# Two-block sequence model on one core: rms norms at the head, between the blocks and at the layer ends rearranged, residual input loaded twice

## What is computed

```python
def rmsnorm(x, g):
    return x * lax.rsqrt(jnp.mean(x * x, axis=-1, keepdims=True) + 1e-6) * g

h = concatenate([meta, x])                     # first block
xn = rmsnorm(h, norm_g)                        # its sections: xn @ w_in
h = h + merged @ w_out
x = rmsnorm(h, final_norm_g)[:, 16:]           # norm 1 between the blocks

h = concatenate([meta_2, x])                   # second block, two layers
u = rmsnorm_2(h, pre_norm_w[l])                # norm 2 between the blocks, when l = 0
h = h + rmsnorm_2(mix @ w_out_2[l], post_norm_w[l])
```

## Time and profile before

| | us |
|---|---|
| median of 3 runs | 3834.13 |
| lowest, highest | 3829.82, 3835.44 |
| the profiled execution, device time | 3825.8 |
| its span in the trace | 3824.0 |
| PE busy | 3630.4 (95%) |
| DVE busy | 1438.7 (38%) |
| ACT busy | 463.9 (12%) |

### The profile page before, as it was taken

The page is one execution under the profiler, slowest core; times in us unless marked ns, Lnnn a source line. Parts: engine busy times, 40 slices in busy tenths (PEclk is TensorE's granted clock), DMA queues, the critical chain, the costliest instruction groups (busy, mean ns, idle before and its releaser), DMA issues.

```text
span 3824.0 us, 46727 instructions
## 1 busy us (share of the span) xinstructions
PE 3630.4 (95%) x19871; PEld 3020.2 (79%) x19871; DVE 1438.7 (38%) x2423; ACT 463.9 (12%) x951; POOL 19.0 (0%) x42
## 2 busy tenths in 40 slices
PE   7999999999999999979999989899789999899997
PEld 5888888888888988868878867677678888777786
DVE  0335431324375534210204654634202026546341
ACT  1011200011011101010000012111100000111111
POOL 0000000000000000000000000000000000000000
PEclk9999899999999999989999999999999999899998
DMA  6442244442434114524444422333424444322431
GB/s 208 139 154 88 86 135 132 135 130 94 155 122 131 47 47 164 181 88 132 132 135 145 140 89 73 98 108 110 144 88 154 135 138 148 101 83 78 129 110 66
DMA packets 424736, 456.29 MB, mean 119 GB/s; under 512 B 14621, under 2 KB 402030, under 8 KB 423758
## 3 DMA queue, kind: packets, MB, share of 16 engines
q1 hardware_dynamic: 422382, 443.19, 36.4%
q0 software_dynamic: 1824, 8.28, 0.6%
q10 hardware_dynamic: 352, 2.23, 0.2%
HBM read 449.35 MB, written 4.33 MB: 119 GB/s over the span
## 4 chain that ended last, share of the span: by engine, by line
PE 90%; DVE 4%; ACT 2%; DVEq 2%; issue 1%; ACTq 0%; DMA 0%; POOL 0%; POOLq 0%
PE bank L1591 32%; PE bank L276 21%; PE bank L350 9%; PE bank L1718 8%; PE bank L383 4%; PE bank L1790 3%; PE bank L1005 3%; DVE tok L431 1%; PE bank L527 1%; PE bank L307 1%; PE bank L1683 1%; PE bank L1777 1%; PE bank L315 1%; PE bank L1666 1%; PE bank L1700 1%
## 5 line engine op out<-in xcount | busy, mean ns | idle before, releaser
L1591 PE MATMUL bank<-xnT,ring 128*128 128x272 f32 (+3 forms) x5632 | 1291.8, 392 | 19.7 <-DVEq L331 19.7
L1591 PEld LDWEIGHTS bank<-xnT,ring 128*128 128x128 f32 (+2 forms) x5632 | 1058.5, 189 | 250.6 <-issue 35.1
L276 PE MATMUL bank<-xnT,ring 128*128 128x272 f32 (+1 forms) x3072 | 690.0, 388 | 11.6 <-DVEq L331 10.9
L276 PEld LDWEIGHTS bank<-xnT,ring 128*128 128x128 f32 x3072 | 585.3, 191 | 115.8 <-issue 13.4
L350 PE MATMUL bank<-xnT,ring 128*128 128x256 f32 x1536 | 345.5, 385 | 0.7 <-ACT wk L1179 0.7
L350 PEld LDWEIGHTS bank<-xnT,ring 128*128 128x128 f32 x1536 | 292.9, 193 | 41.4 <-ACT wk L1179 1.1
L1718 PE MATMUL bank<-G,ring 128*128 128x272 f32 (+1 forms) x1024 | 242.6, 388 | 1.3 <-DVE G L2135 1.3
L1718 PEld LDWEIGHTS bank<-G,ring 128*128 128x128 f32 x1024 | 193.0, 190 | 38.9 <-issue 3.6
L383 PE MATMUL bank<-G,ring 128*128 128x256 f32 x768 | 169.6, 385 | 9.8 <-DVEq L651 5.0
L383 PEld LDWEIGHTS bank<-G,ring 128*128 128x128 f32 x768 | 148.2, 193 | 31.0 <-DVEq L651 5.4
L431 DVE RECIPROCAL G<-G 128x272 f32<-128x272 f32 (+3 forms) x25 | 149.4, 5977 | 1.8
(11 more groups left out here) (456 smaller groups left out, 2656.6 us busy)
## 6 DMA issues: line engine op xcount, KB each, us to landing
ring<-in_w_in SPq DMA_DIRECT2D x156, 2048.0 KB, 8.2
ring<-in_w_out SPq DMA_DIRECT2D x32, 2048.0 KB, 8.4
ring<-in_w_br SPq DMA_DIRECT2D x12, 2048.0 KB, 8.1
ring<-in_w_out SPq DMA_DIRECT2D x16, 1024.0 KB, 11.1
kept<-hT POOLq DMA_DIRECT2D x1, 2176.0 KB, 10.1
hT<-kept POOLq DMA_DIRECT2D x1, 2176.0 KB, 11.9
wk<-in_pool_w POOLq DMA_DIRECT2D x2, 1024.0 KB, 11.1
out<-G SPq DMA_DIRECT2D x2, 1024.0 KB, 5.0
```

The source lines that it names most:

```text
L276: mm = pe.matmul(bank[j][:, first:T], ring[:, s, k, j * P:(j + 1) * P], rhs[:, k, first:T], start=(k == 0), stop=(k == KT - 1))
L1591: mm = pe.matmul(out_, ring[:, s, k, c:c + m], xnT[:, k, first:T], start=(k == 0), stop=(k == KT - 1))
```

## The change

1. **Head.** `x` comes in as rows of 128 tokens (`x_tok`), half by SP and half by ACT, `meta` apart (`m_tok`). The 14 vectors are loaded by POOL. ACT sums the squares of each row while squaring (`accum_out`), DVE does half of the second 128 rows. The norm's factor of each token stands on a diagonal (`diag`), and one matmul of a tile of `x_tok` with it turns and scales at once; DVE multiplies by the gain straight out of PSUM. PE makes the turned tile k+2 between the steps k of the first output tile of the first section (`chasing_section_pe`).
2. **Residual.** No store and no load of `hT`. `x` is loaded again to `x_tok` (`x_back`) by POOL after `rk_free`, and two matmuls with `eye` add it to each tile of `merged @ w_out` in PSUM.
3. **Between the blocks.** ACT squares each tile and copies it to `hT`. DVE keeps two running sums: of the squares, and of the squares times `final_norm_g` squared. Two matmuls each turn the running sums and the last tile into two rows, from which both norms' factors follow. DVE writes `xnT` straight from `hT` with both gains (`gpre`), one `xn_ready` per tile, PE chases, and the 16 products for `hT` come after. The meta tokens' norm and the vectors' transposes stand inside the section, at tiles 4 and 8.
4. **Layer ends and the head of layer 1.** The squares are summed on DVE as well; PE has two matmuls instead of 16 (`acc_own`). PE chases in the first section of layer 1. `Ln` reads PSUM itself, with epsilon as bias, so the DVE step of L324 is gone.

The core of the diff:

```diff
+        def chasing_section_pe(pe, first, ready):
+            for s in range(SLOTS):
+                pe.wait_ge(w_loaded[s], 16 * uses["pe"][s].go())
+                for j in range(2):
+                    pe.wait_ge(proj_free, tiles["pe"].go())
+                    for k in range(KT):
+                        if s == j == 0:
+                            ready(k)
+                        mm = pe.matmul(bank[j][:, first:T], ring[:, s, k, j * P:(j + 1) * P], xnT[:, k, first:T],
+                                       start=(k == 0), stop=(k == KT - 1))
...
         def rms_root_act(act, first=0):
...
+            act.preload_act_table(ACT.Ln)
+            act.activation(row, norm_bank(act)[:, first:T], ACT.Ln, bias=eps[:, 0:1]).then_inc(work_free, 1)
...
-            v.tensor_scalar(sm[:, first:T], b[:, first:T], 1.0 / D, EPS, ALU.mult, ALU.add).then_inc(work_free, 1)
...
+        def block_end_pe(pe):
...
+                for k in range(KT):
+                    pe.matmul(bank[j][:, META:T], ring[:, s, k, j * P:(j + 1) * P], merged[:, k, META:T],
+                              start=(k == 0), stop=False)
+                if t == 0:
+                    pe.wait_ge(S["x_back"], 32)
+                for i in range(2):
+                    mm = pe.matmul(bank[j][:, META + i * P:META + (i + 1) * P], x_tok[i][:, t * P:(t + 1) * P], eye,
+                                   start=False, stop=(i == 1))
...
+                if t == 8:
+                    pe.wait_ge(S["meta_sq"], 1)
+                    for k in range(KT):
+                        mm = pe.matmul(banks["meta"][:, 0:META], ones, squares1[:, k, 0:META], start=(k == 0), stop=(k == KT - 1))
...
+            pe.wait_ge(S["rms_acc"], count["pe"]["rms_acc"].go())
+            for name, acc in (("own", acc_own), ("both", acc_both)):
+                pe.matmul(banks[name][:, META:T], ones, acc[:, META:T], start=True, stop=False)
...
+        def block_end_act(act):
...
+                act.activation(squares1[:, t, META:T], bank[t % 2][:, META:T], ACT.Square, scale=SQ).then_inc(S["rms_sq"], 1)
+                act.activation(hT[:, t, META:T], bank[t % 2][:, META:T], ACT.Copy).then_inc(proj_free, 1)
...
+            act.preload_act_table(ACT.Ln)
+            act.wait_ge(S["rows_in"], 1)
+            act.activation(l_row[:, META:T], c_row[:, META:T], ACT.Ln)
+            act.wait_ge(S["rows_in"], 2)
+            act.activation(n_row[:, META:T], n_row[:, META:T], ACT.Ln, bias=eps[:, 0:1]).then_inc(S["rms_rstd"], 1)
+            act.drain()
+            act.activation(sm[:, META:T], l_row[:, META:T], ACT.Exp, scale=-0.5)
+            act.wait_ge(S["rows_in"], 3)
+            act.activation(c_row[:, META:T], c_row[:, META:T], ACT.Exp, scale=-0.5).then_inc(S["rms_rstd"], 1)
...
+            v.tensor_scalar(c, wbank(work["dve"].n)[:, META:T], EPS, None, ALU.add).then_inc(work_free, 1)
...
+            v.reciprocal(n, c)
...
+            v.tensor_tensor(n, wbank(work["dve"].n)[:, META:T], n, ALU.mult).then_inc(work_free, 1)
...
-                        if 4 * s + j >= 2:
-                            rms_tile_pe(pe, squares, 4 * s + j - 2, m0)
...
+                wait("rms_acc")
+                pe.matmul(b[:, m0:T], ones, acc_own[:, m0:T], start=True, stop=False)
+                wait("rms_sq", KT)
+                pe.matmul(b[:, m0:T], ones, squares[:, KT - 1, m0:T], start=False, stop=True).then_inc(work_full, 1)
...
+            sp.dma_start(x_tok[0], x[0, 0:P, :]).then_inc(S["x0_in"], 16)
...
-            pool.dma_start(kept, flat(hT)).then_inc(S["h_kept"], 16)
...
+                    pool.dma_start(tok[row:row + rows, n * P:(n + 1) * P], src).then_inc(S["stack_in"], 16)
...
+            def turned_input(k):
+                u = turns["pe"].go()
+                pe.wait_ge(turn_free, u)
+                for (t0, n), src, d in zip(TOK_AT, x_tok + [m_tok], diag):
+                    mm = pe.matmul(tbank(u)[:, t0:t0 + n], src[0:n, k * P:(k + 1) * P], d[0:n, 0:n], start=True, stop=True)
+                mm.then_inc(turn_full, 1)
+
+            def input_ready(k):
+                if k + 2 < KT:
+                    turned_input(k + 2)
+                pe.wait_ge(turn_free, k + 3)
...
+            act.activation(junk[0:META, 0:D], m_tok, ACT.Square, scale=SQ, accum_out=ssq[0:META, 3:4]).then_inc(S["x_sq"], 1)
...
+            for i in range(2):
+                v.tensor_scalar(diag[i], eye, rstd3[:, i:i + 1], None, ALU.mult)
...
+            for k in range(KT):
+                v.wait_ge(turn_full, k + 1)
+                v.tensor_scalar(xnT[:, k, :], tbank(k + 1)[:, 0:T], vec("norm_g", 1, k), None, ALU.mult).then_inc(turn_free, 1)
```

354 lines of the change are left out of this document (229 added, 125 removed).

## The result

The changed kernel takes 3765.5 us, the median of four runs from 3763.3 to 3767.4, against 3832.0 for the kernel before beside it: a ratio of 0.983, with a 95% interval from 0.981 to 0.984. The forecast was 3780.6 with a range from 3766 to 3793, so the sign was right and the gain larger than the range allowed. The profiled execution took 3763.3 with a span of 3761.6, against a span of 3824.0 before: 62.4 us shorter, where the sum said 53.5.

The account below looks back on a forecast made before the run. PE bounds the kernel (90% of the last-ending chain). Gains of 10.7 (head), 24.5 (between blocks), 11.5 (layer ends) and 6.8 (layer 1's head) sum to 53.5 us; 3834.1 less that gives 3780.6, range 3766 to 3793.

Parts of the forecast that it names:

- `x` matmuls: Residual in the 16 `w_out` tiles: 32 added PE matmuls with 128 moving columns cost 10.2 us, bounds 6.9 and 11.4.
- The head: Program start to the first output tile: it ends at 44.7 against 55.4, gain 10.7 us, bounds 4 and 17.
- the turned tile: Head: two matmuls with 128 moving columns and one with 16 take 0.90 us, 14.4 for 16 tiles.
- the start at the low clock: Head: cost 1.7 us before the change; the prediction took 2.0.
- Rows 8: Profile rows of the first mixer: four records, two 128-column matmuls, take 0.64 us, used to price small matmuls.
- rival (a): Weight loads hide better: 0.107 per 128-column record, `x` matmuls 6.9 us, turned tile 0.60; total 3772.5; chance 0.14.
- Between the blocks otherwise: Last `w_out` tile to layer 0: pause 47.9 becomes 7.5 us; gain 24.5 after added PE work, bounds 21 and 30.
- Layer ends and the head of layer 1: 13 sums of squares leave PE per layer, gain 11.5 us; layer 1 starts after 3.0 instead of 9.82, gain 6.8.
- Clock: Head of layer 1: clock might stay up over the shorter pause; counted as nothing, worth up to 2.6 us more.
- (b): Head: input lands no earlier, `x` at 16.3, gain 6.4 or nothing, total up to 3791 us; chance 0.10.
- (c): Layer starts: PE waits for several products or DVE falls behind; 2 x 6.3 us lost, total 3793; chance 0.03.
- (d): Head: POOL's small vector loads run one after another, there at 80 us; total 3839 to about 3920; chance 0.02.

Follow-up runs that it names:

- warm_head: Changed kernel plus 20 spare PE matmuls before the vectors and 9 before the first turned tile: 3760.7 us; the same code again 3767.6 us.
- sums_on_pe: Changed kernel with the layer-end sums of squares back on PE, one matmul between output tiles, without DVE's running sum: 3776.8 us.
- one_wait: Changed kernel, but PE waits for all 16 `xn_ready` before the first matmul of layers 0 and 1: 3778.5 us.
- after_again: The changed kernel run once more, unchanged: 3770.2 us.
- warm_early: Changed kernel with only 20 spare matmuls before PE's first wait, none later: 3766.7 us.
- warm_late: Changed kernel with only 4 spare matmuls between the vectors' transposes and the first turned tile: 3768.0 us.
- meta_twice: Changed kernel with each turned tile of the head doing its 16-token matmul a second time: 3782.6 us.
- warm_pauses: Changed kernel plus spare matmuls in three pauses: between the blocks, around layer 1's norm sums, before the output transposes: 3762.6 us.
- three best kernels: Changed kernel with early head fill, meta tokens loaded first and pauses filled; then plus best2's addition; then plus best3's: 3754.7, 3751.4, 3746.6 us.
- meta_dve: Changed kernel with the meta tokens' squares added by one DVE reduction, leaving PE one matmul of 2 records: 3765.6 us.
- best2: Changed kernel with warm_early's fill, meta tokens loaded before x's second half, warm_pauses' fills and meta_dve's reduction: 3751.4 us.
- best3: best2 with 6 more spare matmuls between the vectors' transposes and the first turned tile: 3746.6 us.

## Why the forecast was too high

The median came out 15.1 us below the forecast. 4.0 of it are the basis: 3834.1 was the median of three executions, and 28 of the same kernel have 3830.1. 1.2 are the other side of that: the four runs of the result lie below the eight of their kernel. 9.9 are the sum itself: 3830.1 - 3766.7 = 63.4 against 53.5.

Two steps of the sum failed in the direction of the miss. The price of the small matmuls between the blocks was 3.8 too high, 3.1 of it in the `x` matmuls. And the work that the change leaves alone was put at nothing, where the profiled pair shows 6.8 in the sections and 0.5 in the norm's sums. The head was missed the other way, by 2.0, and the layer ends by 0.2: 3.8 + 7.3 - 2.2 = 8.9, which is 62.4 less 53.5.

Step by step:

**The head, 10.7 forecast, 8.7 measured.** The inputs of the chain were better than written: `diag` at 19.06 and not 21.4, though the meta tokens' load took a place in it that the prediction did not see. At full pace the chase takes 22.6 from its first matmul to the end of the first tile (18.89 to 48.39 - 6.91 in `warm_head`), against 14.4 + 6.9 = 21.3: the turned tile was put too high (0.76, not 0.90), the product step too low (0.63, not 0.43). The parts by themselves, 6 x 0.109 and 2 x 0.216, give 1.09 and not 1.39, so a change of form costs here too; that it is an exposed load of weights, as it looks, was not tried. **The term of the head that failed is the start at the low clock:** 27.7 in the changed kernel (19.06 to 53.66 - 6.91) less 22.6 is 5.1, where the prediction took 2.0 from the start of a dense section before. Reckoned the same way, the eight traces with this head give 4.0 to 7.7. The extra 3.1 and 1.3, less 2.3, make 2.1; missed were 2.0.

**The `x` matmuls, 10.2 forecast, 7.1 measured. The price of a pair is the step that failed.** Rows 8 gave 0.64 for four records, and the prediction took them for the price of the form. They were the price of the form next to a 16-column product; by itself a pair is 0.44, 0.11 a record. The lower bound in the prediction, 6.9, was nearly the value, and rival (a), given 0.14, was right about this term. The Trainium skill's rule, TensorE: Matmul & The Clock Gate, LDWEIGHTS (loading the stationary operand), 107 ns for 128 columns, agrees with the 0.11 per record here, and also with the meta tokens' sum (3.48 / 32 = 0.109), which had been put at 4.1.

**Between the blocks otherwise.** The transposes took 1.09 + 0.37 for 1.6, the gap 7.49 for 7.5. The chain on DVE and ACT was right link by link. With the two terms above the gain is 28.3 and not 24.5, at the favourable end of the stated 21 to 30.

**Layer ends and the head of layer 1.** 11.3 for 11.5, and 6.8 for 6.8; `sums_on_pe` and `one_wait` put both back at their price.

**Clock.** The prediction counted nothing for it and named at most 2.6. In the profiled pair 7.3 us were gained in work that the change leaves alone. The trace's clock records explain 5 to 6 of them: PE worked less at the low level in layer 0's first tiles (5.6 and 4.0 us), the norm's sums of layer 1 (4.3, 3.2), layer 1's head (5.2, 3.4), the rest of layer 1 (33.4, 30.1), its end (4.8, 3.2), and the sections of the first block and layer 0 (77.4, 75.9); half of the 11.0 us of difference is 5.5. The shorter pause at layer 1's head is a cause that was tried: `one_wait` puts it back and loses 0.9 more than the pause. The rest of layer 1's gain repeats in every trace of the changed kernel, but its cause was not found. The first block's gain did not repeat in `after_again`: there low phases move from execution to execution. The other 2 us are not placed.

**The rivals.** (a) named the mechanism and overshot at the turned tile (0.60, measured 0.76); its time, 3772.5, was still too high, for the basis and the clock. (b) fell: `x` was there at 9.4 and the meta tokens at 10.5. (c) fell: DVE kept up, and only `one_wait` shows its 2 x 6. (d) fell: the vectors were turned by 14.5. The ranking by sign, 0.96 for faster, needs no change; the range was cut too near on its fast side, since it left out both the basis and the clock.

## What to carry to other kernels

Take the price of a small matmul from a row in which its neighbours have the form that they will have in your code; 16-column neighbours raised a 128-column pair from 0.44 to 0.64, half by their narrow weights and half by the few columns that they move. Compare with a basis of many executions when single ones scatter by 12 us, and settle terms of a few us in the stretch and not in the median. And look at what queues behind a large transfer on the same engine's queue: a small load put first was worth 1.6 us at the head.

## What the runs showed of the chip that was not expected

- **The granted clock reads 1.00 before its first recorded change.** In the changed kernel the windows at the head show it beside 13 to 16 records in 4 us:

```profile
24.00:28.00 4.00, 4.00 (x13) 3.34 (x14) 1.00 (x2) 0.00 (x0) 0.00 (x0) 1.00 1.10 348
...
32.00:36.00 4.00, 4.00 (x25) 3.40 (x24) 1.49 (x3) 0.00 (x0) 0.00 (x0) 1.00 1.10 348
```

  In `warm_early` the same 14 to 16 records stand beside 0.50. So the half pace at the head is the low level, 1.2 GHz, and the column starts late: it says 1.00 up to the first change, whatever the level is.
- **The way back up is slow and uncertain at the head.** From the first turned matmul, with PE never idle, the half pace lasted 11 us in the changed kernel, 15 in its repeat, and 9 to 17 in the eight traces that share its head. So the 17 of `warm_early` and of `warm_late` lie inside what no fill gives. It was over 40 in `meta_twice`, and absent in `warm_head`, while the same code ran its second time at the low level from 21.6 for 13.7 us. Filling the pauses ahead of it did not decide it. At the pauses later in the program filling worked: in `warm_pauses` and the three best kernels no low phase stands between the blocks or around layer 1's head. The other 13 traces have one of 6.8 us or more at the first place and one of 20.5 us at the second. What in the chase keeps the clock down is open.
- **The clock can fall with PE busy.** In the 16 `w_out` tiles a low phase of 6.8 us, which begins 2.4 us into the 32 records that move 16 columns, stands in 4 of the 14 traces that have these records and in none of the three that do not (`meta_dve`, `best2`, `best3`). The kernel before and the changed one have a much larger one in common. In the first block another 32 records that move 16 columns (L537) are followed by small products, and in all 18 traces a low phase of 23.9 to 27.3 us begins 2.9 to 5.9 us after the first of these records. PE is busy in all or nearly all of it. The changed kernel's row of these records, then a window ahead of it and one inside the low phase:

```profile
416.28 3.79 PE L537 MATMUL bank<-G 128*128 128x16 f32 x32
```
```profile
412.00:416.00 4.00, 4.00 (x20) 3.54 (x19) 2.27 (x2) 0.00 (x0) 0.00 (x0) 1.00 0.00 0
...
436.00:440.00 4.00, 4.00 (x18) 3.85 (x19) 0.00 (x0) 0.48 (x2) 0.00 (x0) 0.50 0.00 0
```

  At half speed its 27.0 us of PE's work cost about 13 us by estimate (half of them), against 4 to 8 at the head. That the 16-column records take the clock down fits both places and is not shown: no run took L537 out, and what follows it is made of small matmuls too.
- **Narrow weights are not cheap.** 16 columns of weights in a row of 128-column ones cost 0.11 us more per head than 128 columns.
